# Band and block attention layers: the first head's scores follow one projection group fewer

## The reference

```python
def sliding_sink_attention(h, w_in, w_out, sinks, rel_table):      # band: 16 query heads, 2 key/value heads
    q, k, v = jnp.split(h @ w_in, [qw, qw + kw], axis=-1)
    o = banded_attention(q, k, v, rel_table, A_WINDOW, sinks)       # causal, window of 128
    return o.reshape(B, S, -1) @ w_out

def moba_attention(h, w_in, w_out, rel_table):                      # block: 16 heads for q, k and v
    q, k, v = jnp.split(h @ w_in, 3, axis=-1)
    ...                                                             # 256 tokens are one block: causal softmax
    return out.transpose(...).reshape(B, S, H * dh) @ w_out
```

## Time and profile before

| | |
|---|---|
| median of 3 runs | 3314.49 us |
| profiled execution, its own time | 3317.67 us |
| its span, first to last instruction | 3315.9 us |
| PE busy, share of the span | 3261.1 us, 98% |
| DVE busy | 2034.8 us, 61% |
| ACT busy | 1743.1 us, 53% |
| mean granted clock of PE | 0.995 of 2.4 GHz |

### The profile page before, as it was taken

One profiled execution on the slowest core, in us unless ns is written; L12 is line 12 of the kernel. 1 busy time (PEld: TensorE's weight loads), 2 busy tenths in 40 slices (PEclk: granted clock), 3 DMA queues, 4 the chain that ended last, 5 costly groups with the idle time before them and its releaser, 6 DMA issues.

```text
span 3315.9 us, 53125 instructions
## 1 busy us (share of the span) xinstructions
PE 3261.1 (98%) x20062; PEld 2893.1 (87%) x20062; DVE 2034.8 (61%) x2777; ACT 1743.1 (53%) x2539; POOL 70.3 (2%) x150
## 2 busy tenths in 40 slices
PE   8999999999999999999999999999999999999999
PEld 7899988888999888888888889888888988888887
DVE  5567565555675656567656567655656665656755
ACT  4457544444674444446545457544445654545644
POOL 0000000000000000000000000000000000000000
PEclk9999999999999999999999999899999999999999
DMA  6666355455653554545545555255555455455454
GB/s 254 219 224 223 141 182 187 179 199 188 222 175 142 186 190 179 190 176 178 197 184 187 185 194 195 83 201 187 195 186 192 163 191 186 183 189 193 163 190 177
DMA packets 105598, 617.93 MB, mean 186 GB/s; under 512 B 10919, under 2 KB 19239, under 8 KB 35560
## 3 DMA queue, kind: packets, MB, share of 16 engines
q1 hardware_dynamic: 85576, 565.52, 46.6%
q10 hardware_dynamic: 19872, 50.34, 4.6%
HBM read 614.71 MB, written 9.50 MB: 188 GB/s over the span
## 4 chain that ended last, share of the span: by engine, by line
PE 91%; DVE 3%; ACT 2%; issue 1%; POOL 0%; ACTq 0%; DMA 0%; POOLq 0%; DVEq 0%; SPq 0%
PE ps L2075 24%; PE ps L2079 12%; PE ps L2210 7%; PE ps L2209 7%; PE ps L2211 7%; PE ps L2191 5%; PE ps L2193 5%; PE ps L2192 5%; PE ps L2150 4%; PE ps L2096 2%; PE ps L2097 2%; PE ps L2098 2%; DVE wlo L1326 1%; PE ps L2579 1%; ACT v L789 1%
## 5 line engine op out<-in xcount | busy, mean ns | idle before, releaser
L1326 DVE TENSOR_TENSOR wlo<-raw,whi 128x2048 fp32r<-128x2048 f32 x435 | 996.5, 2292 | 574.5 <-ACT whi L756 574.1
L2075 PE MATMUL ps<-xhl,whi 128*128 128x512 f32 x3456 | 1202.0, 397 | 0.0
L756 ACT CAST whi<-raw 128x2048 fp32r<-128x2048 f32 x435 | 828.0, 1903 | 145.2 <-PE ps L2211 110.5
L2079 PE MATMUL ps<-xhl,wlo 128*128 128x256 f32 x3456 | 893.6, 279 | 0.0
L2075 PEld LDWEIGHTS ps<-xhl,whi 128*128 128x128 f32 x3456 | 627.5, 188 | 121.6
L2079 PEld LDWEIGHTS ps<-xhl,wlo 128*128 128x128 f32 x3456 | 651.7, 189 | 37.4
L2210 PE MATMUL ps<-wlo,ht 128*128 128x512 f32 x1056 | 417.3, 395 | 0.0
L2209 PE MATMUL ps<-whi,ht 128*128 128x512 f32 x1056 | 417.2, 395 | 0.0
L2211 PE MATMUL ps<-whi,ht 128*128 128x512 f32 x1056 | 416.7, 395 | 0.0
L2191 PE MATMUL ps<-xhl,whi 128*128 128x256 f32 x1360 | 391.7, 288 | 2.4 <-DVE wlo L1326 2.4
L2193 PE MATMUL ps<-xhl,wlo 128*128 128x256 f32 x1360 | 385.8, 284 | 0.0
(11 more groups left out here) (318 smaller groups left out, 3857.5 us busy)
## 6 DMA issues: line engine op xcount, KB each, us to landing
raw<-stream SPq DMA_DIRECT2D x528, 1024.0 KB, 4.8
bias<-rel_bias ACTq DMA_DIRECT2D x80, 256.0 KB, 2.6
gain<-gains ACTq DMA_DIRECT2D x18, 1024.0 KB, 4.8
bias<-fixed_bias ACTq DMA_DIRECT2D x40, 256.0 KB, 2.8
rel_bias<-rel_vectors SPq DMA_DIRECT2D x16, 512.0 KB
x<-x_tokens SPq DMA_DIRECT2D x2, 512.0 KB, 6.5
gain<-gains SPq DMA_DIRECT2D x1, 512.0 KB, 7.9
y_tokens<-x SPq DMA_DIRECT2D x1, 512.0 KB, 2.6
```

The source lines that it names most:

```text
L756: nc.scalar.copy(whi[:, slot, :], raw[:, slot, :]).then_inc(sem["hi_ready"], 1)
L1326: nc.vector.tensor_tensor(wlo[:, slot, :], raw[:, slot, :], whi[:, slot, :].bitcast(F32), ALU.subtract).then_inc(sem["lo_ready"], 1)
L2075: wide = lambda: pe.matmul(ps[:, bank, 0:2 * half], hi[:, k, col0:col0 + P], src[:, k0 + k, :], start=first and k == 0, stop=last and k == ...
L2079: e = pe.matmul(ps[:, bank, 0:half], lo[:, k, col0:col0 + P], src[:, k0 + k, 0:half], start=False, stop=False)
```

## The change

`early` goes from 3 to 2 in the band layers and from 4 to 3 in the block layer. The group that is no longer done ahead (group 2 in the band layer, the queries of heads 4 to 7; group 3 in the block layer, likewise the queries of heads 4 to 7) goes into the table of slots in front of what stood there. Its four quarters, and what turn 0 had already, fill turn 0, behind head 0's scores: 5 quarters in place of 1 in the band layer, 6 in place of 2 in the block layer. From turn 1 on the slots are the same. On ACT and DVE the step that was cast and subtracted whole beside that group is now done in four quarters within turn 0.

```diff
-GQA_SLOTS = slots_of([part for j in range(3, 8) for part in quarters(j)][:-1], [1] * 19)
-MOBA_SLOTS = slots_of([part for j in range(4, 15) for part in quarters(j)][:-1],
-                      [2, 2, 2, 2, 3, 3, 3, 3, 3, 3, 3, 3] + [2, 2, 2, 2, 1, 1, 1])
+GQA_SLOTS = slots_of([part for j in range(2, 8) for part in quarters(j)][:-1], [5] + [1] * 18)
+MOBA_SLOTS = slots_of([part for j in range(3, 15) for part in quarters(j)][:-1],
+                      [6, 2, 2, 2, 3, 3, 3, 3, 3, 3, 3, 3] + [2, 2, 2, 2, 1, 1, 1])
...
-            weave("gqa2", "window", 0, f("kv", 0, 1) + f("q", 0, 4), 3, GQA_SLOTS,
+            weave("gqa2", "window", 0, f("kv", 0, 1) + f("q", 0, 4), 2, GQA_SLOTS,
                   sink=PRM["sink2"] + (i // 3) * HEADS)
...
-            weave("moba", "causal", 0, by_four, 4, MOBA_SLOTS)
+            weave("moba", "causal", 0, by_four, 3, MOBA_SLOTS)
```

## The result

The changed kernel takes 3337.45 us in the median of 6 runs (3333.27 to 3340.07), the kernel before 3314.61 (3312.61 to 3319.43, 6 runs). The ratio is 1.0062, with a 95% interval of 1.0051 to 1.0073: 0.5 to 0.7% slower. Forecast were 3334, in a range of 3326 to 3343.

A forecast was written before the change was run, and what follows sets the result against it. PE, busy 98%, was taken as the bound. Band layers 10.0, block layer 5.1 and clock 4.5 sum to 19.6 us: 3337.3 us for the profiled execution, 3334 against the median, range 3326 to 3343.

The forecast's parts named there:

- The gate opens at 1508.53 after the change too: First band layer: head 0's scores start no earlier, so PE's wait there grows from 0.65 to about 6.5 us.
- the second turning 5.0 us later: Each band layer: second turning of probabilities moves from 1516.58 to 1521.6; 10.0 us for the two layers.
- a wait of 1.2 us of its own: Band layers, second turning: PE arrives at 1520.4 but waits for the probabilities' copy until 1521.6.
- the chain of eight links: Band layers: ACT and DVE steps from the moved group's end to the second turning, from cast to PE, 6.6 us.
- 5.1 us later for the third turning: Block layer: a 5.5 us gate wait, then the moved group and 14.0 us of chain; third turning about 2574.2 against 2569.07.
- one low stretch for each gate: Behind each of three gates PE's clock falls to 1.2 GHz, costing 1.5 us each, 4.5 in all; chance 0.62.
- one case, a wait of 2.17 us in the sparse layer: PE's wait up to 2009.49, followed by granted clock 0.50 and 0.66; 13 products short, or 1.4 us.
- The clock did not stay up: Rival at the new waits: low stretches fall into the waits or don't come; +15.1 us, 3330; chance 0.16.
- low for 10 us at each gate: Rival: clock stays low longer, 4.9 us each in place of 1.5; +25 to 30, 3340 to 3345; chance 0.15.
- Nothing was given back later in the layers: Rival: later waits in the stages absorb the backlog, bringing the loss to +6 us or less; chance 0.04.
- The rival with the faster kernel: Band layers: gate opens when PE gets there, 2.5 us gained in each, kernel at 3309.5; chance 0.03.
- the wait at the first turning: Band layers: PE's 1.86 us wait for the first exponentials goes, as DVE does less ahead of head 0.

The follow-up runs named there:

- the run with PE busy: Changed kernel with 48 unused products (40 in the block layer) given to PE in each gate's wait; 3332.40 us.
- the half run: Changed kernel with two of the moved group's four quarters kept ahead of head 0's scores on PE; 3328.43 us, ratio 1.003.
- PE's order alone: PE's order of the changed kernel, with ACT and DVE ordered as in the kernel before; 3337.84 us, ratio 1.0054.
- the gate opened earlier: Changed kernel, with ACT and DVE making the keys' and first queries' parts ahead of group 3's step in the band layers; 3335.63 us.
- the second set: The changed kernel measured once more, without further edits; 3337.08 us, ratio 1.006.
- ACT's and DVE's order alone: ACT and DVE ordered as in the changed kernel, with PE ordered as in the kernel before; 3322.59 us, ratio 1.0011.
- DVE early: Kernel before with only DVE's order changed: earlier head 0 scaled scores (band layers), one low part a turn later in each layer; 3318.29 us, ratio 0.9998.

## Why the prediction was right

**What bounds the kernel, and the gate.** "The gate opens at 1508.53 after the change too": it opened 12.6 us behind the first product of group 1 in both. The waits were 6.37 and 6.38 us in the band layers (forecast 6.4) and 5.27 in the block layer (5.3). That DVE's chain holds the gate was argued before; the run with that chain in another order shows it for the band layers. In the block layer the gate's wait is ended by the same kind of row (L1562), and its chain was not changed in a run.

**The waits in the band layers.** Forecast: the second turning 5.0 us later, with a wait of 1.2 us of its own; with the clock up it came 5.3 later, and its wait was 1.29. From the gate to that turning the sum has 13.1 us and the run with PE busy 13.4: the moved group's end came 0.2 us later, and the chain of eight links, taken from rows one by one, is 0.2 short.

**The block layer.** Forecast 5.1 us later for the third turning; with the clock up 5.6. The moved group ended 0.2 us later than counted, and the links behind it took 14.3 us in place of 14.0.

**The clock.** The forecast has one low stretch for each gate, at 1.5 us. Each gate had one, and it cost 1.3 to 2.3 us: 5.4 us in all in the changed kernel's first trace and 6.4 in its second, where the sum had 4.5. This is the term that was mis-sized; with the 1.1 us by which the waits came out longer it makes the three layers 21.6 and 22.6 us later in place of 19.6.

I had priced it by one case, a wait of 2.17 us in the sparse layer. That was part luck. The same wait, 2.18 us, left the clock at 1.00 in the changed kernel's first trace (its rows stand at the end), so on that trace the price would have been nothing. Nor is the price larger because the wait is: 6.37 us cost 1.3 in one trace and 2.3 in another, and the 3.53 us of the half run cost some 2.7 (5.1 of its band layer less 2.4 for the waits). It goes by how much of the low stretch is left when PE starts again. That all three gates would be hit rested on the same case. It held in both traces of the changed kernel and in those of PE's order alone and the gate opened earlier; in the half run it held at two gates of three.

**Against the rivals.** The clock did not stay up (that would have been 3330; the run with PE busy, 3332, is that case), nor was it low for 10 us at each gate (3340 and more). Nothing was given back later in the layers: the second turning and the end of the first band layer are late by the same 6.6 us. The rival with the faster kernel named the one real gain of the change, the wait at the first turning (1.86 us as the prediction counts it, 1.68 in its row). It was made, in both band layers, and it is in the sum; the gate's wait is three times as long.

**The sum against the profiled execution.** Forecast 19.6 us, the three layers together 21.6, the two profiled executions 15.6, the medians 22.8 and in the second set 19.4. The three layers are the change. The rest of the profiled difference is the stretch with the sparse layer, some 6 us shorter in the changed kernel's first trace; its clock differs from execution to execution. So the forecast of 3337.3 us for the profiled execution, which took 3333.27, missed by something that the change has no part in.

## What to carry to other kernels

Before work is moved from in front of a wait to behind it, ask who opens the gate. Here DVE does, at a moment that does not depend on the moved work, so all 5.7 us of it turned into idle time in the band layers and 5.3 in the block layer. When an engine is busy for 98% of the time, a wait of some us is best filled with work, and where there is none, even with products that nobody needs: DVE's low parts in a later place and 47 such products together made this kernel 0.35% faster. And an engine should not stand in front of a result that is late while other work is queued behind it; move the step to where its input is there.

## What was new about the hardware

- The length of a wait alone does not say whether PE's clock falls behind it. After 2.29 us (the run with ACT's and DVE's order alone) and after 1.73 (DVE early, first band layer) it went to 0.50; after 2.40 (half of the group ahead, block layer) and 1.68 (before; over all of the 8 us behind it, where the earlier trace rows end 0.7 us behind) it stayed at 1.00. Even one and the same wait goes both ways. The one of 2.2 us in the sparse layer has 0.50 behind it in the kernel before, and in the changed kernel, where nothing near it was edited, this:

```profile
2014.75 0.36 PE L2810 MATMUL ps<-k,q 128*128 128x256 f32 x1 [2.18 <-DVE k L1880]
```

```profile
2015.00:2019.00 4.00, 3.67 (x31) 3.46 (x30) 3.86 (x9) 0.00 (x0) 0.00 (x0) 1.00 0.31 129
```

- Products of 128x256 in the wait kept it at 1.00 in all three gates, at no cost of their own: the gates opened at 12.6 and 17.1 us with and without them.
- The clock's falls in the sparse layer make most of the scatter between the profiled executions. The stretch with that layer took from 959.7 to 968.6 us in kernels that are the same there. The granted clock from 1970 to 2150 us was 0.97 where it took 959.7, 0.92 where it took 965.9 (the kernel before) and 0.91 where it took 968.6; over 180 us the 0.06 between the ends is some 11 us at most, against the 9 measured. So the totals of two profiled executions can differ by 9 us with no edit between them; the three layers, of 75 to 120 us each, repeat within 1.
